# Inverse factors of a gated delta net transposed by VectorE in 32x32 blocks, squares and gate rows as fp32r passes

## What is computed

```python
def l2norm(t):
    tf = t.astype(jnp.float32)
    return tf * lax.rsqrt(jnp.sum(tf * tf, -1, keepdims=True) + NORM_EPS)

def gated_delta_rule(q, k, v, g, beta):
...
    gc = jnp.cumsum(g, -1)
    diff = gc[..., :, None] - gc[..., None, :]
    decay = jnp.where(lower, jnp.exp(jnp.where(lower, diff, 0.0)), 0.0)
    kb = k * beta[..., None]
    L = jnp.where(strict, jnp.einsum('bhnid,bhnjd->bhnij', kb, k) * decay, 0.0)
    rhs = jnp.concatenate([v * beta[..., None], kb * jnp.exp(gc)[..., None]], -1)
    sol = lax.linalg.triangular_solve(L + jnp.eye(C, dtype=L.dtype), rhs, left_side=True,
                                      lower=True, unit_diagonal=True)
```

## Time and profile before

| | before |
|---|---|
| median of 3 runs | 2718.45 us |
| lowest, highest | 2718.34, 2719.01 us |
| profiled execution, span | 2717.0 us |
| profiled execution, own time | not recorded apart from its span |
| TensorE busy | 2678.4 us (99%) |
| VectorE busy | 1909.8 us (70%) |
| ScalarE busy | 1212.6 us (45%) |
| GpSimd busy | 854.2 us (31%) |

### The profile page before, as it was taken

One profiled execution on the slowest core, in us unless ns is written; L12 is line 12 of the kernel. 1 busy time (PEld: TensorE's weight loads), 2 busy tenths in 40 slices (PEclk: granted clock), 3 DMA queues, 4 the chain that ended last, 5 costly groups with the idle time before them and its releaser, 6 DMA issues.

```text
span 2717.0 us, 45293 instructions
## 1 busy us (share of the span) xinstructions
PE 2678.4 (99%) x17387; PEld 2250.4 (83%) x17387; DVE 1909.8 (70%) x2190; ACT 1212.6 (45%) x1572; POOL 854.2 (31%) x646
## 2 busy tenths in 40 slices
PE   6999999999999999999999999999999999999998
PEld 4798998899898888888888888889777778888887
DVE  1476777787787687666666666588999997655554
ACT  2355455545546445333333333354433334444344
POOL 1076676676667412600000000004565550000000
PEclk9999999999999999999999999999999999999999
DMA  9966666676665676666666666655555556666664
GB/s 364 354 219 207 227 225 204 223 239 200 224 229 188 219 223 228 189 187 186 187 190 188 190 186 186 185 162 172 171 179 170 161 173 187 192 186 186 192 202 155
DMA packets 283976, 552.53 MB, mean 203 GB/s; under 512 B 16882, under 2 KB 54323, under 8 KB 282675
## 3 DMA queue, kind: packets, MB, share of 16 engines
q1 hardware_dynamic: 263488, 473.49, 56.5%
q0 software_dynamic: 19472, 76.06, 7.4%
q10 hardware_dynamic: 866, 0.80, 0.1%
HBM read 548.19 MB, written 2.10 MB: 203 GB/s over the span
## 4 chain that ended last, share of the span: by engine, by line
PE 96%; DMA 2%; DVE 1%; SPq 1%; ACT 0%; issue 0%; DVEq 0%
PE pg L1220 40%; PE pd L1220 18%; PE pg L936 13%; PE pg L923 6%; PE pg L1207 4%; PE pg L955 3%; PE pd L849 2%; DMA wr<-in_gdn_w_in 1%; PE pd L1096 1%; PE pd L1078 1%; PE pd L1415 1%; PE pd L1428 1%; DMA arena<-in_mod_w 1%; PE pg L849 1%; PE pd L1027 1%; PE pd L1010 1%
## 5 line engine op out<-in xcount | busy, mean ns | idle before, releaser
L2341 DVE TENSOR_TENSOR wl<-wr,wh 128x1024 fp32r<-128x1024 f32 x615 | 773.7, 1268 | 453.7 <-ACT wh L1818 451.2
L1818 ACT ACTIVATE wh<-wr 128x1024 fp32r<-128x1024 f32 x616 | 652.8, 1061 | 936.2 <-PE pg L1220 590.3
L662 POOL TENSOR_TENSOR wl<-wr,wh 128x1024 fp32r<-128x1024 f32 x195 | 478.9, 2458 | 366.3 <-ACT wh L1599 231.3
L1220 PE MATMUL pg<-wh,hh 128*128 128x512 f32 x1344 | 529.8, 394 | 0.3 <-DVE hl L2414 0.3
L1220 PE MATMUL pg<-wl,hh 128*128 128x512 f32 x1344 | 527.3, 392 | 0.0
L1220 PE MATMUL pg<-wh,hl 128*128 128x512 f32 x1344 | 525.7, 391 | 0.0
L1599 ACT ACTIVATE wh<-wr 128x1024 fp32r<-128x1024 f32 x216 | 227.7, 1057 | 356.4 <-PE pg L936 196.4
L1220 PEld LDWEIGHTS pg<-wh,hh 128*128 128x128 f32 x1344 | 252.6, 188 | 59.1 <-DVE wl L2341 2.4
L936 PE MATMUL pg<-hh,wh 128*128 128x256 f32 x1024 | 300.7, 294 | 0.8 <-ACT arena L1659 0.8
L1220 PEld LDWEIGHTS pg<-wh,hl 128*128 128x128 f32 x1344 | 252.5, 188 | 56.3
L1220 PEld LDWEIGHTS pg<-wl,hh 128*128 128x128 f32 x1344 | 252.3, 188 | 53.9
(11 more groups left out here) (446 smaller groups left out, 4727.3 us busy)
## 6 DMA issues: line engine op xcount, KB each, us to landing
wr<-in_w_in SPq DMA_DIRECT2D x224, 512.0 KB, 3.8
wr<-in_ffn_w_gu SPq DMA_DIRECT2D x176, 512.0 KB, 3.8
wr<-in_gdn_w_in SPq DMA_DIRECT2D x128, 512.0 KB, 4.1
arena<-in_mod_w POOLq DMA_DIRECT2D x60, 1024.0 KB, 6.7
wr<-in_ffn_w_down SPq DMA_DIRECT2D x88, 512.0 KB, 4.6
arena<-in_mod_w SPq DMA_DIRECT2D x32, 1024.0 KB, 13.7
wr<-in_gdn_w_in SPq DMA_DIRECT2D x128, 256.0 KB, 3.1
wr<-in_gdn_w_out SPq DMA_DIRECT2D x56, 512.0 KB, 4.5
```

Source lines behind the costliest of these rows:

```text
L662: nc.gpsimd.tensor_tensor(wl[c % RING][:], wraw[c % 4], wh[c % RING][:].bitcast(F32), ALU.subtract)\
L1220: m = nc.tensor.matmul(halves(bank)[:, h, :], act[x][:, k0 + k, h * P:(h + 1) * P], w[s][:, k, :], skip_group_check=True, start=(first and ...
L1818: a(wh[c % 4][:], wraw[c % 4], ACT.Copy).then_inc(s_hc, 1)
L2341: v.tensor_tensor(wl[c % 4][:], wraw[c % 4], wh[c % 4][:].bitcast(F32), ALU.subtract).then_inc(s_lc, 1)
```

## The change

**Transposed factors.** TensorE no longer flips a factor for the levels 2 to 16 nor at the opening. VectorE's transpose works in blocks of 32x32 (`STREAM_TRANSPOSE`, 128x512 per call), and what it makes of `Tc` is the transposed factor in place for the blocks on their own half; `Us` (the right half of `Ub`) takes it. ScalarE then copies the two halves that a crossed product reads from the other partitions, 64x256 each, from `Us` to `Uc` (`cross(s)`). Products read `Us` or `Uc` by block (`u_block`). At the opening the mask product goes into `Us`, and `Tc` is its transpose. s=2 uses the crossed pattern of the later levels. At s=32 TensorE still flips in fp32.

**Squares.** VectorE squares into `aTb`; ScalarE makes an fp32r Square of q and k (`squares_high`) behind `silu_v`; VectorE subtracts one from the other; TensorE sums high and low part in four fp32r matmuls.

**Gate rows.** The gates are split once, at setup, into high and low part (`gparts`, 4 x 32 partitions); GpSimd's product covers 128 partitions, and TensorE makes two fp32r matmuls with 64 rows.

```diff
-PEO = order("ssq", "rows", "gram", "ktok", "t2", "x2", "tx2", "u2", "x4", "tx4", "u4", "x8",
...
+PEO = order("ssq", "rows", "gram", "ktok", "vt1", *[f"{a}{s}" for s in LEVELS for a in ("x", "tx")],
+            "u32", "x64", "ux64", "v0", "md0", "s", "o0", "r", "qs", "v1", "o1", "md1")
...
                 for n in range(2):
-                    m = nc.tensor.matmul(pd[0][:, n * 512:(n + 1) * 512], ones[:], sqb[:, n * 512:(n + 1) * 512],
-                                         start=True, stop=True)
+                    for i in range(2):
+                        m = nc.tensor.matmul(pd[0][:, n * 512:(n + 1) * 512], ones_r, sq_s[i][:, n * 512:(n + 1) * 512],
+                                             start=(i == 0), stop=(i == 1))
...
-                    r = slice(NH * n, NH * (n + 1))
-                    m = nc.tensor.matmul(pd[0][:, n * 512:(n + 1) * 512], ones[r, :],
+                    r = slice(2 * NH * n, 2 * NH * (n + 1))
+                    m = nc.tensor.matmul(pd[0][:, n * 512:(n + 1) * 512], ones_r[r, :],
...
-                V("lm")
                 Ac("kg")
...
+                def u_block(b, n):
+
+                    r = slice(64 * (n % 2), 64 * (n % 2) + 64)
+                    return Us[r, n, :] if n % 2 == b else Uc[r, n // 2, :]
...
-                flip_blocks(pd[0], Uc, slot)
...
-                    if s < 32:
-                        for m in range(4):
-                            t = tr(pd[par][:, m * P:(m + 1) * P], Tc[:, 2 * m:2 * m + 2, :])
-                    else:
+                    if s == 32:
...
+            def squares_high(g):
+
+                act.wait_ge(s_qk, g + 1)
+                a(sq_s[0][:], fl(qk), ACT.Square).then_inc(s_sqh, 1)
...
+                def cross(s):
+
+                    V(f"us{s}")
+                    a(Uc[0:64, 0:4, :], heads(Us)[64:P, :, 0, :], ACT.Copy)
+                    a(Uc[64:P, 0:4, :], heads(Us)[0:64, :, 1, :], ACT.Copy).then_inc(s_a, 1)
+                cross(1)
...
                     silu_qk(it + 1)
                     silu_v(it + 1)
+                    squares_high(it + 1)
...
-                fq = qk.rearrange("p a b -> p (a b)")
-                v.tensor_tensor(sqb, fq, fq, ALU.mult).then_inc(s_sq1, 1)
+                fq, sq = qk.rearrange("p a b -> p (a b)"), fl(aTb)
+                link(v.tensor_tensor(sq, fq, fq, ALU.mult))
+                dve.wait_ge(s_sqh, it + 1)
+                v.tensor_tensor(sq_s[1][:], sq, sq_s[0][:].bitcast(F32), ALU.subtract).then_inc(s_sq1, 1)
...
-                PEw("t2")
-                done(v.tensor_tensor(heads(Tc), identc.unsqueeze(1).unsqueeze(1).broadcast_to([P, 4, 2, 64]),
-                                     by_n(compact(pd[0])), ALU.subtract))
                 dve.wait_ge(s_v, bv + VO["lm"])
-                done(v.tensor_tensor(Uc, identc.unsqueeze(1).broadcast_to([P, 8, 64]), Uc, ALU.subtract))
+                done(v.tensor_tensor(Us, identc.unsqueeze(1).broadcast_to([P, 8, 64]), Us, ALU.subtract))
+                dve.wait_ge(s_v, bv + VO["us1"])
+                done(v.transpose(Tc, Us))
...
+                    done(v.tensor_tensor(heads(Tc), heads(Tc), by_n(compact(pd[0])), ALU.subtract))
+                    if s < 32:
+                        dve.wait_ge(s_v, bv + VO[f"t{s}"])
+                        done(v.transpose(Us, Tc))
```

More of the change, by code:

```diff
@@ L219, in build @@
         zt = take(8, P)
+        xb_at = at[0]
         Xb = take(8, P)
@@ L239, in build @@
         Sb = take(VH, P)
-        rowm = take(VH, P)
-        take(8)
-        take(VH * P - 8)
+        rowm_at = at[0]
+        take(VH, P)
+        gpart_at = at[0]
+        take(P)
+        take(VH * P - P)
         tk = take(7, NH)
@@ L1053, in each_block @@
                         yield from ((0, 2 * m), (1, 2 * m + 1), (0, 2 * m + 1), (1, 2 * m))
-                def flip_blocks(bank, src, at):
-                    for n in range(8):
-                        for b in range(2):
-                            r = slice(64 * b, 64 * b + 64)
-                            m = nc.tensor.matmul(block(bank, b, slot(n)), src[r, at(n), :], ident[r, r],
-                                                 start=True, stop=True)
-                    return m
-                flip_blocks(pd[0], Uc, slot)
                 for h in range(VH):
@@ L1077, in x_step @@
                             r = slice(64 * b, 64 * b + 64)
-                            m = nc.tensor.matmul(block(pd[par], *crossed(s, b, n)), lTb[r, n, r], Tc[r, n, :],
+                            m = nc.tensor.matmul(block(pd[1], *crossed(b, n)), lTb[r, n, r], Tc[r, n, :],
                                                  start=True, stop=True)
@@ L1086, in delta @@
                     V(f"x{s}")
[L1087 to L1090 removed]
+                    Ac(f"u{s // 2}")
+                    if s == 2:
                         Ac("vtok")
[L1092 removed]
                     for b, n in each_block():
[L1094 removed]
+                        half, i = crossed(b, n)
                         r = slice(64 * half, 64 * half + 64)
[L1096 removed]
+                        m = nc.tensor.matmul(block(pd[0], b, slot(n)), u_block(b, n), Xc[r, i, :], start=True, stop=True)
                     m.then_inc(s_pe, 1)
@@ L1122, in delta @@
                     u = Ub[r, n, 64:P] if n % 2 else Uc[r, n // 2, :]
-                    m = nc.tensor.matmul(block(pd[par], 0, slot(n)), Xc[r, n // 2, :], u, start=True, stop=True)
+                    m = nc.tensor.matmul(block(pd[1], 0, slot(n)), Xc[r, n // 2, :], u, start=True, stop=True)
                 m.then_inc(s_pe, 1)
-                assert par == 1
                 yield
```

91 lines of the change are left out of this document (42 added, 49 removed).

## The result

The changed kernel takes 2781.68 us (median of 4 runs, 2777.81 to 2783.41) against 2718.41 of the kernel before: ratio 1.023, 95% interval 1.0216 to 1.0243. Forecast were 2691 us, and the range ended at 2710.

The account below looks back on a forecast made before the run. TensorE, busy 99% of the span, was taken as the bound. Savings of 31.0 and 4.9 less losses of 5.9 and 2.4 gave -27.6 from the 2717.0 span; with 1.45 added, 2691 us, range 2683 to 2710.

Parts of the forecast that it names:

- rows: Gate rows on TensorE: two fp32r passes replace four, saving 0.70 per batch in seven batches, 4.9 us.
- opening and s=2: TensorE at each batch's opening: the dropped 64x64 flip saves 1.16, the crossed pattern for s=2 saves 0.92.
- a level's flip: TensorE in levels 2 to 16: each flip left out saves 0.45, four levels 1.80 per batch.
- The transposition: VectorE's block transpose of 128x512: taken as 0.69, between bounds of 0.69 and 2.21.
- The end of the batch: Square and new subtraction delay the transposes of "on" by 0.84 at seven ends, 5.9 us lost, if VectorE goes first.
- batch 0: First batch: the new subtraction waits behind GpSimd's, making the convolution some 3.3 later; 2.4 us booked as lost.
- From the level's rows I read about 2 us between the factor's arrival and TensorE's need of it, so nothing is booked: Levels: about 2 us of slack hides VectorE's transpose and ScalarE's crossed copies; no loss counted.
- VectorE's 2.8 per batch: VectorE in the levels: net added work from transposes less a dropped PSUM operation, 2.8 per batch, booked at nothing.
- the product is then ready about as TensorE reaches it: Levels: the mask's second operation may wait for GpSimd as before, yet its product comes in time; nothing booked.
- GpSimd first at the end of a batch: Rival: GpSimd's subtraction goes ahead of VectorE's rstd product, transposes 3.1 late instead of 0.84; 2705 us, chance 0.32.
- the transposes fill VectorE: Rival in the levels: transposes of up to 2.21 each exceed the 2 us slack; slower, 2736 us, chance 0.07.
- 31.0 + 4.9 us: TensorE's forecast savings: 31.0 from levels, opening and s=2 over eight batches, 4.9 from gate rows over seven.

Follow-up runs that it names:

- pool_half: The changed kernel with GpSimd subtracting only 512 of 1024 columns in each split of the projection's weights (half of each low part left out): 2690.42 us.
- the shift: The changed kernel with the pairs of mod products one step later and GpSimd's loads one chunk later: 2749.59 us; the same shift was also tried on other variants.
- no_sq: The changed kernel with the squares as before (no Square on ScalarE, no subtraction, two fp32 matmuls): 2769.76 us.
- extra_tr: The kernel before with four more VectorE block transposes per batch that nobody reads, TensorE still flipping: 2732.26 us, ratio 1.0049.
- no_sq_shift: The changed kernel with the squares as before, the pairs of mod products one step later and GpSimd's loads one chunk later: 2725.64 us.
- flips_back: The changed kernel with TensorE's four 128x128 transposes back at levels 2 to 16, into a place nobody reads: 2771.39 us.
- its control: The kernel before with GpSimd's splits of the projection's weights on 512 of 1024 columns: 2717.47 us, ratio 0.9995.

## Why the prediction was wrong

**What held.** The terms of TensorE's savings in the levels and rows, measured where the batch kept its pace: rows 0.64 per batch (0.70 forecast); opening and s=2, 95.95 to 93.83, 2.12 (1.16 + 0.92 = 2.08); a level's flip 0.44 (0.45). The transposition 0.71 (0.69). The end of the batch 0.78 late (0.84), VectorE first. pool_half, with all of the change's instructions, takes 2690.4 where I said 2691. That the totals meet within 1 us is partly luck: the batches are 92.3 where I said 92.8, and batch 0 is 0.6 longer than before where I had it 1.5 shorter. But it is the sum, within these errors, for a kernel in which VectorE and GpSimd hardly disturb each other.

**What failed** is the step "From the level's rows I read about 2 us between the factor's arrival and TensorE's need of it, so nothing is booked". I looked at the slack of one result, the factor. What came late most was another, the mask product behind the pair (45.1 of the waits), and the factor came late as well (13.1 + 4.3); I hadn't asked what stands around the transposition in VectorE's queue. The rows to ask were there: pairs of 1.53 to 3.2 in the levels of the kernel before, depending on where a split stood, so the length of a pair was a matter of position, and I was about to shift every position. I had that mechanism in hand and used it at the end of the batch only. In the prediction's own terms, VectorE's 2.8 per batch were booked at 0, and the six batches behind batch 0 came out at 105.0 on the average instead of 92.8, 12 us more. The pair at the opening and the loads' place are about half of that (99.0 with the shift), and the squares 0.9 (104.2 in no_sq); the rest was not taken apart further.

**At the opening** "the product is then ready about as TensorE reaches it" held for the first product; but the pair behind the transposition took 5.3, and the next product waited 2.0. The runs with the shift, which frees this place and moves the loads too, come out 19 to 44 us lower.

**Batch 0** was mis-sized: 2.4 booked, 6.8 measured for the squares alone. It came out at 110.4 instead of 96.9, and it is long in other variants too (106.7 in extra_tr, without the squares' change); why it is longer than the later ones stays open.

**The clock** was no term at all. 19 us more of TensorE's busy time came with the waits (2659.4 against 2640.0), most of it because the granted clock fell behind some of them (0.66 in 505 to 510).

**A slip in the sum:** with GpSimd first at the end of a batch the rstd product would be done at 350.5 + 2.52 + 1.31 = 354.3 and not 354.0, so 3.4 late and not 3.1. That rival would have been 2707 us; it didn't happen.

**The rival** "the transposes fill VectorE" named the right engine and sign, with a chance of 0.07, and a wrong rule: it charged a transposition for its own length, and so decided only from 1.78 on. At 0.71 it came true all the same, in sign. The Trainium skill, "SBUF — State Buffer", section Who interferes with whom, says that the port pair that VectorE and GpSimd share is an exclusive lock, that a VectorE instruction with two SBUF inputs contends for it with a GpSimd instruction that reads SBUF, and that the order of issue decides who blocks. The traces agree (pairs of 1.53 in pool_half against 3.5 here, where a split comes between). I had cited it and applied it to the end of the batch only.

**What stays open.** Which of the two kinds of batch an execution falls into (no_sq_shift 2717.6 to 2734.9, flips_back 98.2 or 104.6 per batch) wasn't predicted by anything that I found. That pairs and splits holding each other up make the loss is shown by pool_half with its control; that the position of the pairs matters fits the shifts, which moved the loads as well. A version that keeps them apart by a semaphore, or that places the pairs so that GpSimd's loads still come in time, wasn't tried.

## What to carry to other kernels

When work moves from the bound engine to one with idle time, list what stands behind it in that engine's queue, and whether those instructions share something with a third engine; the moved instruction's own length is the smaller part of its price. A queue that is 77% busy on average can be full in the stretch that counts (here 9.15 of 9.27 us), and making the bound engine faster there may take away the very slack that kept two others out of each other's way. Then take the savings one at a time: here about two thirds of TensorE's forecast savings could be had (24 of 31.0 + 4.9 us) by moving one pair of products with its loads, keeping the flips at levels 2 and 4, and leaving the squares as they were.

## What I had not expected of the hardware

- Blocked time is recorded as busy time: VectorE 2036.5 against 1873.5 us for the same 2235 instructions. Of a busy share of 84%, as in the stretch shown, a part is waiting.
- Taking work from TensorE and giving it to VectorE made the kernel slower, and giving TensorE its transposes back as well, to no use, did not make it slower still (flips_back: 2771.4 against 2781.7 us by the medians, ranges that just touch).
- The same split of 128x1024 takes GpSimd 2.40 and VectorE 1.23 us.
- A pair that had started, 0.06 us ahead of the split (537.74 and 537.80), was not through with it: the split came in between its two products, and the pair took 3.5 us instead of 1.5.
